# Sharing the product of keys and query between VectorE and GpSimd in a one-core decoder-layer kernel

## The reference

```python
def _sb_logits(q, k, bias):
    z = jnp.einsum('bqhd,bkhd->bhqk', q, k, preferred_element_type=jnp.float32) * SB_SCALE
    return z + bias.astype(jnp.float32)[None, :, None, None]
...
    k_past = k_pool[layer][page_table].reshape(b, past, SB_HEADS, SB_HEAD_DIM)
    z = jnp.concatenate([_sb_logits(q, k_past, bias), _sb_logits(q, k_new, bias)], axis=-1)
```

## Time and profile before

| | |
|---|---|
| median of 3 runs | 1771.85 us |
| lowest and highest | 1770.38 and 1779.13 us |
| profiled execution, its own time | 1780.09 us |
| its span | 1778.5 us |
| TensorE busy | 1559.8 us (88%) |
| VectorE busy | 599.8 us (34%) |
| ScalarE busy | 279.7 us (16%) |
| GpSimd busy | 180.5 us (10%) |
| moved by DMA | 533.84 MB, 300 GB/s over the span |
| mean granted clock of TensorE | 0.941 |

### The profile page before, as it was taken

How to read it: one execution, slowest core, us unless ns; L and a number is a source line. 1 busy time by engine, 2 the same in 40 slices (tenths; PEclk the granted TensorE clock), 3 DMA queues, 4 the chain that set the end, 5 groups by cost and what they waited for, 6 DMA issues and landing times.

```text
span 1778.5 us, 20970 instructions
## 1 busy us (share of the span) xinstructions
PE 1559.8 (88%) x7762; PEld 822.4 (46%) x7762; DVE 599.8 (34%) x888; ACT 279.7 (16%) x538; POOL 180.5 (10%) x285
## 2 busy tenths in 40 slices
PE   7976777778899997889999999999999999999993
PEld 5765534446777775444333433333333233333331
DVE  2699633057544445321122112212121221112124
ACT  1100232103311111211111111110110111011102
POOL 5422232102032112000000000000000000000000
PEclk9987888879989998889999999999999999999997
DMA  8798687765311005549999999999999999999991
GB/s 298 253 320 317 232 276 257 264 239 163 102 18 48 29 21 178 192 148 409 410 410 410 410 410 410 410 410 410 410 410 410 410 410 410 410 410 410 410 410 50
DMA packets 157497, 533.84 MB, mean 300 GB/s; under 512 B 8591, under 2 KB 9674, under 8 KB 157410
## 3 DMA queue, kind: packets, MB, share of 16 engines
q1 hardware_dynamic: 143442, 487.61, 70.4%
q0 software_dynamic: 14000, 45.53, 7.7%
HBM read 528.65 MB, written 4.46 MB: 300 GB/s over the span
## 4 chain that ended last, share of the span: by engine, by line
PE 64%; DMA 19%; DVE 8%; issue 5%; ACT 2%; POOL 1%; SPq 1%; POOLq 0%; DVEq 0%; ACTq 0%
PE bank L727 62%; DMA projT<-in_w_gate_up 16%; DMA ring<-in_w_in 2%; PE bank L728 2%; DVE ring L1589 1%; DMA ring<-in_w_mem_kv 1%; DVE ring L1678 1%; DVE arena L1680 0%; ACT memT L1535 0%; DMA ring<-in_cache_sb_k 0%; DVE arena L1795 0%; DVE arena L1797 0%; DVE arena L1796 0%; ACT arena L1340 0%; SPq L446 0%
## 5 line engine op out<-in xcount | busy, mean ns | idle before, releaser
L727 PE MATMUL bank<-arena 128*128 128x128 f32 (+9 forms) x2172 | 370.2, 360 | 56.8 <-DMA projT<-in_w_gate_up 17.3
L727 PEld LDWEIGHTS bank<-arena 128*128 128x128 f32 (+3 forms) x2172 | 247.0, 187 | 185.3 <-issue 105.9
L727 PE MATMUL bank<-projT,ring 128*128 128x264 f32 x1056 | 266.0, 408 | 31.3 <-DMA ring<-in_w_in 22.5
L727 PE MATMUL bank<-ring,memT 128*64 128x512 f32 (+2 forms) x1152 | 278.5, 596 | 16.3 <-ACT memT L1535 15.2
L727 PEld LDWEIGHTS bank<-projT,ring 128*128 128x128 f32 x1056 | 207.5, 201 | 78.2 <-issue 23.3
L727 PE MATMUL bank<-projT 128*64 128x512 f32 (+1 forms) x1056 | 239.0, 593 | 2.8 <-DMA projT<-in_w_gate_up 2.8
L727 PE MATMUL bank<-ring,projT 128*64 128x512 f32 x1024 | 232.2, 595 | 1.4
L1974 DVE TENSOR_SCALAR arena<-bank 128x256 f32<-128x256 f32 x64 | 27.2, 425 | 504.7 <-PE bank L727 504.7
L727 PEld LDWEIGHTS bank<-ring,memT 128*64 128x64 f32 (+2 forms) x1152 | 88.1, 140 | 169.4 <-issue 143.1
L727 PEld LDWEIGHTS bank<-projT 128*64 128x64 f32 (+1 forms) x1056 | 75.6, 141 | 139.4 <-issue 133.0
L727 PEld LDWEIGHTS bank<-ring,projT 128*64 128x64 f32 x1024 | 70.7, 137 | 146.5 <-issue 142.4
(11 more groups left out here) (271 smaller groups left out, 976.5 us busy)
## 6 DMA issues: line engine op xcount, KB each, us to landing
ring<-in_w_gate_up SPq DMA_DIRECT2D x64, 2048.0 KB, 23.3
projT<-in_w_gate_up SPq DMA_DIRECT2D x64, 2048.0 KB, 23.2
ring<-in_w_down SPq DMA_DIRECT2D x64, 2048.0 KB, 23.4
ring<-in_w_in SPq DMA_DIRECT2D x13, 2048.0 KB, 8.6
ring<-in_cache_sb_k SPq DMA_DIRECT2D x64, 256.0 KB, 5.6
ring<-in_cache_sb_k POOLq DMA_DIRECT2D x64, 256.0 KB, 5.8
ring<-in_cache_sb_v SPq DMA_DIRECT2D x64, 256.0 KB, 5.3
ring<-in_cache_sb_v POOLq DMA_DIRECT2D x64, 256.0 KB, 5.5
```

Of the source, the lines that this page charges most:

```text
L727: mm = lambda out, l, r, first, last, **k: pe.matmul(out, l, r, start=first, stop=last, **k)
```

## The change

GpSimd multiplies two of the eight pages of each K slab with the query. It can't read the query from PSUM, so ScalarE copies each sample's query to SBUF first (`copy_query`), into `pvm`, two buffers in turn; the third and later copies wait until GpSimd is through with the buffer's last query. VectorE multiplies pages 0 to 5, waits for GpSimd's product, and sums all eight. In GpSimd's program the product of K(i) stands ahead of the page loads of K(i+2).

```diff
+            def scale_keys(i):
+
+                g.wait_ge(sem("q_copied"), i // 2 + 1)
+                arrived(g, ("K", i))
+                k = slot(("K", i)).rearrange("p (n f) -> p n f", n=8)[:, 6:8]
+                g.tensor_tensor(k, k, pvm[i // 2 % 2].unsqueeze(1).to_broadcast([P, 2, W5]), ALU.mult).then_inc(sem("k_scaled"), 1)
+
             g.wait_ge(sem("pages_in"), 16)
             second_half(("K", 0))
             second_half(("K", 1))
...
-            second_half(("K", 2))
-            second_half(("K", 3))
+            for i in range(2):
+                scale_keys(i)
+                second_half(("K", i + 2))
             link(g.tensor_tensor(m_up[:], tri_lt[:], blk[:], ALU.mult))
...
             g.sem_inc(sem("masks"), 1)
-            for i in range(4, 16):
-                second_half(("K", i))
+            for i in range(2, 16):
+                scale_keys(i)
+                if i < 14:
+                    second_half(("K", i + 2))
...
+            def copy_query(b_):
+
+                q = take(act, ("qb", b_))
+                if b_ >= 2:
+                    act.wait_ge(sem("k_scaled"), 2 * b_ - 2)
+                act.activation(pvm[b_ % 2], q[:, :], ACT.Copy).then_inc(sem("q_copied"), 1)
...
+                if ft % 4 == 0 and ft:
+                    copy_query(ft // 4 - 1)
                 move(("p", ft), pT[:, ft, :], lambda b: b[:, 0:T])
+            copy_query(7)
...
-                    prod_ = tt_(k, k, q[:, :].unsqueeze(1).to_broadcast([P, 8, W5]), ALU.mult)
+                    v.wait_ge(sem("q_copied"), b_ + 1)
+                    prod_ = tt_(k[:, 0:6], k[:, 0:6], q[:, :].unsqueeze(1).to_broadcast([P, 6, W5]), ALU.mult)
...
+                    v.wait_ge(sem("k_scaled"), 2 * b_ + half + 1)
                     v.tensor_reduce(zs[:, b_, 8 * half:8 * half + 8, :], slot(name).rearrange("p (n h d) -> p n h d", n=8, h=SBH),
                                     AX.X, ALU.add).then_inc(sem("k_used"), 1)
```

## The result

The changed kernel is slower: 1787.09 us median of 10 runs (1777.26 to 1790.19), against 1775.77 us for the kernel before in its 10 runs (1768.61 to 1780.33). The ratio is 1.0059 with a 95% interval of 1.0040 to 1.0078, so 7 to 14 us. The profiled execution of the changed kernel took 1786.24 us, its span is 1784.6.

A forecast was written before the change was run, and what follows sets the result against it. It took the chain of VectorE's K sums, slab loads and TensorE up to mkv0 as the bound; delays from GpSimd's queue reach +18.4 us, 1798.5 on the profiled execution, 1790 on the median of 1771.85; range 1779 to 1803.

The forecast's parts named there:

- Step 1: Sum over K1: GpSimd's product 1 waits for K2's loads, so the sum ends at 63.3 us, not 54.7; nothing added.
- Step 2: Sum over K3: K3's loads, masks, product 2, K4's loads and product 3 in line end it at 94.6 us; +14.8.
- K3's loads, out 5.3 us after product 1: GpSimd's queue before the masks: 1.3 us, 3 x 1.15 and 0.54 after the product, so out at 64.1 us.
- Step 3: win4 to the sum over K7: late win4, TensorE, K8's loads and product 7 end it at 139.9 us; +15.4.
- Step 4: win6 to mkv0's issue: load, TensorE, K12's loads, product 11 and sum over K11 put it at 179.0 us; +18.4.
- Step 5: From mkv0's issue on: load 14.86 us and TensorE 30.07 as before, VectorE's end covered; shift stays +18.4 us.
- Five products on the path: K slabs: GpSimd's products 1, 2, 3, 7 and 11 make up 12.0 us of the +18.4.
- the rival that loads collide less: K stage: win4 lands in 10.25 us, products take 1.8, and only the masks hurt; +10, 1782 us; chance 0.09.
- the masks alone hurt: GpSimd's queue: claim, paired with fewer load collisions, that only the masks cost; together +10, 1782 us, chance 0.09.
- The faster rival: K slabs: only VectorE's pace counts, 1.07 us back per slab, 17.1 us for all 16, 1755 us; chance 0.03.

The follow-up runs named there:

- the run with tiny products: Changed kernel, same queue order, but GpSimd multiplies only 8 of each page's 512 numbers: 1782.76 us, ratio 1.0042 to the kernel before.
- the paired products: Changed kernel with two GpSimd products ahead of the page loads of the next two slabs, masks unmoved: 1774.83 us, ratio 1.0005 to the kernel before.

## Why the prediction was right, and where its sum was off

It forecast slower, 1790 us in a range of 1779 to 1803, by the order of GpSimd's queue; 1787.09 lies in it, and the mechanism is the one that was named. But the shift was 10.5 us by the ratio and 10.0 in the stage, where the sum had +18.4: below the forecast's own +13 to +24, and at the lower of its bounds, +10. That 1787 comes so near to 1790 is partly luck, as the base was too low: 1771.85 was the median of three runs, that of ten is 1775.77. By its own steps:

- *The parts.* VectorE's product 3.34 us (3.3 forecast), GpSimd's 2.36 (2.4), ScalarE's copy 0.60 on no path. All right. The Trainium skill ("GPSIMD Engine Reference", section "Elementwise — side-by-side cycle accounting") has 4,497 ns for 2,048 elements; half of it, the estimate of 2.25 us, was 0.1 short of the measured 2.36.
- *Step 1.* The sum over K1 ended at 62.75 (63.3 forecast), and TensorE's win3 began no later than before, 72.28 against 72.72. Right.
- *Step 2, +14.8.* Measured 91.44 - 79.79 = +11.65. The term "K3's loads, out 5.3 us after product 1" was mis-sized: 2.35 us after the product's end (58.22 to 60.57), because their preparation runs beside it. They were out at 60.57, not later than before (61.05), so the masks and product 2 came 3.3 us sooner than forecast. K4's loads were out at 82.01 instead of 87.8 for the same reason. With that, product 3 was off the path, and what led to the sum over K3 was VectorE's own row of work behind product 2: sum K2, product K3, sum K3. Even by the forecast's own times the two tied (product 2 at 82.5, then 4.4 and 3.3 us of VectorE's, is 90.2, where product 3 ended), so it was a mistake to count product 3 as a link, though it did not move the sum.
- *Step 3, to +15.4.* Measured +8.8 (133.26 - 124.46). win4's load was kept at the 15.8 us that it had taken; it took 13.1. TensorE took 16.23 us over win4, not 17.46, though it had stood idle for 16.4 us before it and not 7.5; the longer idle time did not make it slower. The rest was as forecast: K8's loads out 5.5 us after TensorE's end (5.2), product 7 right behind, then the sum.
- *Step 4, to +18.4.* Measured +12.65, so this step added 3.8 where 3.0 were forecast.
- *Step 5, the old course from there.* mkv0's load took 12.2 us instead of the 14.86 kept, which gives back 2.6: +10.0. VectorE's end was covered: its last sum ended at 208.49, forecast 214, and ScalarE came at 221.63.

So the miss of 8.4 us is 3.2 for loads that were charged behind a product, 3.4 for win4 (its load and TensorE's pace) and 2.6 for mkv0's load, less 0.8 in step 4. "Five products on the path" failed by the run with tiny products: three. The loads of win4 and mkv0 went the way of the rival that loads collide less, which had a chance of 0.09; its price, +10, fits, but only in part for its reasons: product time was the forecast's, and the waits for TensorE counted as much as they should have. That the masks alone hurt is ruled out by the paired products, which took off 7.1 us with the masks in place. That win4 and mkv0 landed quicker because less was moved beside them shows in the busy time by stage over each load, win4's before and after, then mkv0's (columns as in the earlier trace rows):

```profile
79.81:95.56 15.75, 8.31 (x42) 7.04 (x40) 6.29 (x2) 1.17 (x3) 5.65 (x11) 0.87 1.01 362
91.47:104.58 13.11, 0.00 (x0) 0.00 (x0) 13.04 (x4) 0.00 (x0) 6.44 (x9) 0.50 0.98 358
...
160.64:175.50 14.86, 0.00 (x0) 0.00 (x0) 13.24 (x4) 0.00 (x0) 2.68 (x5) 0.58 1.04 387
173.29:185.51 12.22, 0.00 (x0) 0.00 (x0) 12.15 (x4) 0.00 (x0) 4.88 (x6) 0.50 1.03 385
```

The DMA engines are full and move the same GB/s before and after, so 5.7 MB pass in the long loads and 4.7 in the short ones, of which 2.1 are the slab itself. The 1.0 MB between them is what four pages hold. Why less of the pages fell into these stretches is not shown.

The faster rival named the right condition, GpSimd's order: with the masks out of the way and no product behind a load that waits, the change does pay, 0.6% with the masks' own 0.2%. It was wrong on the size: 6.4 us of stage and not 17.1, since SyncE's queue then takes over as the bound.

## What to carry to other kernels

When work is given to an engine that also issues loads, read its queue as one line: for each new instruction, what stands ahead of it and what that waits for. Here products of 2.36 us made VectorE wait 44.7 us, and the same products take 0.6% off the kernel before, 0.2% of it the masks' own, in an order in which nothing ahead of them waits for a late slot. And a one-off block of set-up work in such a queue belongs in a stretch where the engine is idle: begun 29 us sooner (at 31.5 instead of 60.6), it took 12 us off the changed kernel and 2.7 us off the stage of the old one.

A load's duration is not a constant to carry over: for the same 2 MB win4 took 15.8, 13.1 or 9.8 us and win6 10.25, 13.1 or 9.7, by what was moved beside them, and more than once a sooner issue was partly paid back by a longer load.

## What the runs showed of the hardware

GpSimd's product has the length 0.228 us for 16 elements, 2.36 for 1,024 and 3.44 for 1,536, that is 2.1 ns an element on top of some 0.2 us, and within 1.5% of itself at all 16 places. VectorE's product and sum kept 3.34 and 4.42 us whether GpSimd multiplied beside them or not (beside it the product at 37.16 and the sum at 87.02, alone the product at 44.89 and the sum at 40.55). VectorE reads the query from PSUM here, and no run has it read from SBUF.

The 3.9 us by which the span grew less than the stage lie in the RWKV-7 loop, whose code the change doesn't touch: its first group of GpSimd products starts 10.4 us later than before (508.12 against 497.71), its last 6.5 (635.07 against 628.56). Busy time by stage of its two middle quarters, first in the kernel before, then in the changed one:

```profile
540.00:584.00 44.00, 39.72 (x284) 34.01 (x282) 19.03 (x35) 7.18 (x15) 12.45 (x11) 0.92 0.13 49
584.00:628.00 44.00, 39.72 (x281) 34.08 (x279) 18.88 (x35) 6.78 (x14) 8.02 (x5) 0.92 0.14 48
```

```profile
550.00:592.00 42.00, 37.73 (x292) 32.07 (x290) 19.57 (x37) 7.18 (x15) 12.42 (x11) 1.00 0.14 51
592.00:634.00 42.00, 37.73 (x272) 32.23 (x272) 18.22 (x33) 6.78 (x14) 8.03 (x5) 0.96 0.15 51
```

The same work takes 44 us at a granted clock of 0.92 and 42 at 0.96 to 1.00. From one of these groups of GpSimd products to the next, the second and third passes took 43.7 and 43.9 us before and 41.2 and 42.6 in the changed kernel, and in all eight profiles between 41.2 and 43.9. What sets the pace of a pass is not shown. Over two passes it is a third of the effect studied, so the stage's end tells more here than one execution's span.
